# A chunked state-space layer: the inner matrices' transfers move from ScalarE to SyncE, and VectorE scans before it makes factors

## The reference, cut to what matters

```
u, z = split(h @ w_in, 2)                  # 512 x 2048 each
states = scan(lam_bar, b_bar @ u)          # 128 groups of 16 channels, 64 complex states each
y  = real(c @ states) + d * u
y  = gelu(y)
y  = y * sigmoid(y @ w_glu + b_glu)        # "glu"
out = (y * silu(z)) @ w_out
```

## Time and profile before

| | us |
|---|---|
| median of 3 runs | 1753.06 (1750.89 to 1755.3) |
| the profiled execution, its own time | 1754.76 |
| its span | 1752.8 |
| TensorE busy | 1678.9 (96%) |
| VectorE busy | 1008.3 (58%) |
| ScalarE busy | 676.2 (39%) |
| GpSimd busy | 590.2 (34%) |

### The profile page before, as it was taken

The page is one execution under the profiler, slowest core; times in us unless marked ns, Lnnn a source line. Parts: engine busy times, 40 slices in busy tenths (PEclk is TensorE's granted clock), DMA queues, the critical chain, the costliest instruction groups (busy, mean ns, idle before and its releaser), DMA issues.

```text
span 1752.8 us, 22905 instructions
## 1 busy us (share of the span) xinstructions
PE 1678.9 (96%) x9216; PEld 1341.5 (77%) x9216; DVE 1008.3 (58%) x1524; ACT 676.2 (39%) x965; POOL 590.2 (34%) x203
## 2 busy tenths in 40 slices
PE   7999999999999998999999999998999999999997
PEld 6777788888788886777788877686677788887876
DVE  4256545686988889985563654897963222222123
ACT  5473223334344355445333323425663322222122
POOL 1422013343633342000244432333774344443432
PEclk8999999999999999999999999998999999999999
DMA  5223002335655665555744322112002233332322
GB/s 165 83 96 96 1 11 89 95 96 143 154 119 136 139 141 106 105 115 163 244 135 128 88 70 73 48 43 85 2 1 73 79 90 96 96 96 74 100 83 81
DMA packets 267566, 168.14 MB, mean 96 GB/s; under 512 B 88875, under 2 KB 247814, under 8 KB 267334
## 3 DMA queue, kind: packets, MB, share of 16 engines
q1 hardware_dynamic: 240544, 142.80, 30.2%
q10 hardware_dynamic: 26614, 22.25, 4.8%
q0 software_dynamic: 304, 1.65, 0.3%
HBM read 145.15 MB, written 16.78 MB: 92 GB/s over the span
## 4 chain that ended last, share of the span: by engine, by line
PE 79%; DVE 11%; ACT 3%; issue 2%; DMA 2%; ACTq 1%; POOL 1%; SPq 0%; DVEq 0%; POOLq 0%
PE PS L700 22%; PE PS L701 22%; PE PS L702 22%; DVE ring_lo L1960 2%; PE PA L896 1%; PE PA L893 1%; ACTq L1621 1%; PE PA L874 1%; PE PS L1260 1%; PE PS L1272 1%; PE PA L1106 1%; PE PA L1244 1%; POOL ring_lo L2639 1%; DVE PB L2563 1%; ACT ring_hi L1382 1%
## 5 line engine op out<-in xcount | busy, mean ns | idle before, releaser
L2639 POOL TENSOR_TENSOR ring_lo<-ring,ring_hi 128x2048 fp32r<-128x2048 f32 (+2 forms) x93 | 405.6, 4361 | 965.9 <-ACT ring_hi L1382 965.5
L1382 ACT ACTIVATE ring_hi<-ring 128x2048 fp32r<-128x2048 f32 (+2 forms) x123 | 223.2, 1821 | 209.5 <-PE PS L702 171.8
L700 PE MATMUL PS<-U3h,ring_hi 128*128 128x512 f32 x352 | 140.0, 398 | 3.1 <-POOL ring_lo L2639 3.1
L701 PE MATMUL PS<-U3l,ring_hi 128*128 128x512 f32 x352 | 140.6, 399 | 0.0
L702 PE MATMUL PS<-U3h,ring_lo 128*128 128x512 f32 x352 | 139.5, 396 | 0.0
L2599 DVE TENSOR_TENSOR SF<-PS,rs 128x512 f32<-128x512 f32 x22 | 15.2, 691 | 166.7 <-PE PS L702 166.6
L700 PE MATMUL PS<-HT5h,ring_hi 128*128 128x512 f32 x256 | 106.3, 415 | 3.0 <-DVE ring_lo L1960 2.9
L1960 DVE TENSOR_TENSOR ring_lo<-ring,ring_hi 128x2048 fp32r<-128x2048 f32 x30 | 91.6, 3065 | 27.6 <-ACT ring_hi L1382 27.6
L702 PE MATMUL PS<-HT5h,ring_lo 128*128 128x512 f32 x256 | 101.4, 396 | 0.0
L701 PE MATMUL PS<-HT5l,ring_hi 128*128 128x512 f32 x256 | 101.2, 395 | 0.0
L1870 ACT ACTIVATE SF<-SF 128x512 f32<-128x512 f32 x22 | 13.9, 632 | 179.1 <-DVE SF L2599 179.1
(11 more groups left out here) (486 smaller groups left out, 4224.9 us busy)
## 6 DMA issues: line engine op xcount, KB each, us to landing
ring<-in_gla_w_in SPq DMA_DIRECT2D x20, 1024.0 KB, 5.2
ring<-in_s_w_in SPq DMA_DIRECT2D x16, 1024.0 KB, 5.8
ring<-in_s_w_glu SPq DMA_DIRECT2D x16, 1024.0 KB, 5.9
ring<-in_w_gate SPq DMA_DIRECT2D x22, 512.0 KB, 4.0
ring<-in_w_up SPq DMA_DIRECT2D x22, 512.0 KB, 5.3
ring<-in_w_down SPq DMA_DIRECT2D x16, 704.0 KB, 4.4
ring<-in_w_in SPq DMA_DIRECT2D x9, 1024.0 KB, 5.2
ring<-in_gla_w_out SPq DMA_DIRECT2D x8, 1024.0 KB, 5.8
```

Source lines behind the costliest of these rows:

```text
L700: pe.matmul(dst, w[0], x[0], start=start, stop=False)
L701: pe.matmul(dst, w[0], x[1], start=False, stop=False)
L1382: act.activation(ring_hi[:, n % NSLOT, 0:plan.size[n]], ring[:, n % NSLOT, 0:plan.size[n]], ACT.Copy)\
L2639: pool.tensor_tensor(ring_lo[:, n % NSLOT, at], ring[:, n % NSLOT, at], ring_hi[:, n % NSLOT, at].bitcast(F32), ALU.subtract).then_inc(wlo ...
```

## The change

ScalarE keeps the 8 issues for batch 0. For batches 1 to 15 they move into a new function `inner_rows(b)` of SyncE, first in `beside_batch(b)`, ahead of `u_loads(b + 1)` and `factor_loads(b + 3)`, with the waits that ScalarE had. VectorE scans first; `b_factors(b + 2)` now stands behind the low parts and the second tile, ahead of the state factors. In batch 15 TensorE has the second tile (`glu_a` 11) whole before `outputs(15)`, and half of `glu_a` 12 between `outputs(15)` and `by_feature(15)`. The instructions are the same in kind and number.

```diff
--- before.py
+++ after.py
@@ -1037,17 +1037,20 @@
                 if b == GA + 2:
                     by_feature(b - 1)
 
-                k = KD if b == GA + 1 else 6
+                k = KD if b in (GA + 1, NBATCH - 1) else 6
                 dense(*beside[1], 0, k)
                 outputs(b)
                 if b + 1 < NBATCH:
                     inside(b + 1)
+                else:
+                    dense(*S5_LAST[0], 0, 4)
                 dense(*beside[1], k, KD)
                 if b != GA + 1:
                     by_feature(b)
                 if len(beside) > 2:
                     dense(*beside[2], 0, KD)
-            for stage, m in S5_LAST:
+            dense(*S5_LAST[0], 4, KD)
+            for stage, m in S5_LAST[1:]:
                 dense(stage, m, 0, KD)
             for i, tile in enumerate(tiles["s5_glu"]):
                 w = parts_view(tile.loads[0], (KD, 2 * P))
@@ -1612,13 +1615,12 @@
                     ins = act.activation(GS[0:SGRP].rearrange("p (r q) m -> p q r m", q=4)[:, q],
                                          PA[32 * q:32 * q + SGRP, 1, 0:2 * P].rearrange("p (r m) -> p r m", r=2), ACT.Copy)
                 ins.then_inc(gs_ready, 1)
-                act.wait_ge(gs_ready, b + 1)
+
                 if b == 0:
+                    act.wait_ge(gs_ready, 1)
                     act.wait_ge(km_zero, 2)
-                if b >= 2:
-                    act.wait_ge(y_ps, b - 1)
-                for t in range(TB):
-                    act.dma_start(KM[b % 2][t * SGRP:(t + 1) * SGRP, :, t * SGRP:P], GS[0:SGRP, :, 0:P - t * SGRP]).then_inc(km_in[b % 2], 16)
+                    for t in range(TB):
+                        act.dma_start(KM[0][t * SGRP:(t + 1) * SGRP, :, t * SGRP:P], GS[0:SGRP, :, 0:P - t * SGRP]).then_inc(km_in[0], 16)
 
             def outputs_of(b):
 
@@ -2306,8 +2308,6 @@
             dve.wait_ge(xt_out, 16)
             link(dve.memset(M[:].rearrange("p g n -> p (g n)"), 0.0))
             for b in range(NBATCH):
-                if b + 2 < NBATCH:
-                    b_factors(b + 2)
                 scan(b)
                 own_tiles = [tile for tile in BESIDE[b] if tile[0] != "glu_a"]
                 for tile in own_tiles[:1]:
@@ -2324,6 +2324,8 @@
                     low_weights(n)
                 for tile in own_tiles[1:2]:
                     scaled(*tile)
+                if b + 2 < NBATCH:
+                    b_factors(b + 2)
                 if b + 2 in DVE_STATES:
                     state_factors(b + 2)
                 for tile in own_tiles[2:]:
@@ -2722,8 +2724,20 @@
                 for s in range(TB):
                     sp.dma_start(UB[s * SGRP:(s + 1) * SGRP, b % 2], src[s]).then_inc(ub_in[b % 2], 16)
 
+            def inner_rows(b):
+
+                sp.wait_ge(gs_ready, b + 1)
+                if b == 1:
+                    sp.wait_ge(km_zero, 2)
+                if b >= 2:
+                    sp.wait_ge(y_ps, b - 1)
+                for t in range(TB):
+                    sp.dma_start(KM[b % 2][t * SGRP:(t + 1) * SGRP, :, t * SGRP:P], GS[0:SGRP, :, 0:P - t * SGRP]).then_inc(km_in[b % 2], 16)
+
             def beside_batch(b):
 
+                if b >= 1:
+                    inner_rows(b)
                 if 1 <= b and b + 1 < NBATCH:
                     u_loads(b + 1)
                 if b + 3 < NBATCH:
```

## The result

| | before | after |
|---|---|---|
| median of the runs, us | 1753.83 (8 runs) | 1746.72 (8 runs, 1740.12 to 1749.51) |
| ratio to before | | 0.9955, 95% interval 0.9941 to 0.9969 |
| span of the profiled execution | 1752.8 | 1744.1 |

The change made the kernel faster by 0.45%, 7.9 us by the ratio. The forecast was 1744.1 us, 9.0 less than before.

A forecast was written before the change was run, and what follows sets the result against it. TensorE, busy 96% of the span, was taken as the bound, with VectorE setting the pace from scan 9. Gains of 7.4 us to `outputs(14)` and 1.6 in batch 15 gave 1753.06 - 9.0 = 1744.1 us; eight-in-ten range 1740 to 1751.5.

The forecast's parts named there:

- Batches 0 to 7: Factors no longer stand ahead of the scan, so TensorE's waits for `M` and low parts go: 4.5 us gained.
- The covers: Factors made late in loop b are ready 2.2 us (even b) and 3.3 us (odd b) before batch b + 1 wants them.
- The new wait: Batch 8 to 9: factors of batch 10 meet GpSimd's last state factors, so TensorE waits 3.9 us.
- The chain of VectorE: Scan 9 to 14: both rotation waits go, leaving 98.2 us of work, plus 3.8 for a fifth factor set: 102.0.
- The clock: After the 3.9 us of idling TensorE loses 1.3 us to the lower clock; 0.65 us reach the chain.
- That rival: Clock stays down longer: TensorE loses 4.3 us, the last `z` tile holds VectorE 3.7; gain 5.9, 1747.2 us; chance 0.12.
- Batch 15: Rotations and scan in time, six more matmuls before `outputs(15)`: the 1.46 us wait goes, 1.6 us gained.
- The sum on 9.0: 7.4 us gained up to `outputs(14)` plus 1.6 in batch 15 make 9.0 us.
- ScalarE's relief is hidden: Rival: copies and rotations late from other work, so waits of 5.5 and 1.6 stay; gain 1.9, 1751.2 us; chance 0.08.
- Inner matrices late: Rival: `KM` takes 10 us in SyncE's queue, four even batches wait 3.1 us each; 1756.5 us; chance 0.05.
- Factors late everywhere: Rival: two more GpSimd meetings delay factors before `b_to_rows(b + 1, 0)`, batches 1 to 8; 14.8 us lost, 1758.9; chance 0.11.

The follow-up runs named there:

- e6: The whole change, but VectorE instead of GpSimd makes the state factors of batch 10; median 1741.50 us, ratio to before 0.9929.
- e5: The whole change, but the factors of batch 10 stand ahead of scan 8; median 1742.12 us, ratio to before 0.9926.
- e1: Against before, only the 8 issues of `KM` move from ScalarE to SyncE; median 1748.01 us, ratio 0.9962.
- e2: Against before, only VectorE's order changes: scan first, factors of b + 2 behind the second tile; median 1748.84 us, ratio 0.9971.
- e4: The whole change without its TensorE part in the last batch; median 1746.66 us, ratio to before 0.9958.
- e7: The whole change, but SyncE issues `KM` behind `UB` and the factors' inputs; median 1760.48 us, ratio to before 1.0036.
- e8: The whole change, but VectorE makes the first two factor instructions twice in loops 0 to 7; median 1760.88 us, ratio to before 1.0032.
- e9: e5, but ScalarE makes the first product of `turns` for batches 11 to 15; `turns` moves behind the low parts; 1738.00 us, ratio to before 0.9907.
- e3: Against before, only TensorE's last batch changes; median 1752.17 us, ratio 0.9992.

## Why the prediction was right, point by point

All measured times count from `additions(0)`; predicted ones are those of the prediction.

| step | predicted | measured |
|---|---|---|
| batches 0 to 7, gain | 4.5 | 4.4 at `additions(8)` |
| wait before `b_to_rows(10, 0)` | 3.9 | 3.84 |
| scan 9, in the times of before | 671.4 | 671.65 |
| wait before `b_to_rows(11, 0)` | 4 to 5 | 4.32 |
| VectorE's wait for the `z` tile | 0.65 | 1.04 |
| scan 9 to scan 14 | 102 to 103 | 103.3 |
| gain at `outputs(14)` | 7.4 | 6.6 |
| gain in batch 15 | 1.6 | 1.8 |
| sum | 9.0 | 8.4 |

- **Batches 0 to 7** went as written: no wait for `M`, none for low parts, none for factors. The covers were 1.7 to 2.8 and 3.6 to 4.0 us where I had 2.2 and 3.3. But the argument that GpSimd's pieces "are mostly over" when the factors come did not hold: the factors met them in every one of these loops, for 1.6 to 3.3 us each time.
- **The new wait** was the step with the most in it, a meeting with GpSimd put into a new place, and it came out to 0.1 us. e6 shows the cause by taking GpSimd away, e5 shows that it lay on the path.
- **The chain of VectorE** held: the sum 98.2 + 3.8 was right. Its story was not, as e1 and e2 showed. I wrote that both waits for rotations go because ScalarE is relieved, and that a set of factors is then added. With the relief alone (e1) both waits go too, but TensorE passes on only about 1.1 us of the second; with the order alone (e2) the added set fills it.
- **The clock** was undersized: TensorE lost 1.6 us behind the first wait, where I took 1.3, and 0.4 us more reached the chain than the 0.65. That rival's price, 3.7, was not reached in any profile, but e4 came to 2.2.
- **Batch 15** had the right size, by luck, and the wrong cause. I gave it to the rotations and six more matmuls together; the relief gives 1.6, the matmuls 0.2.
- **The sum on 9.0** is 0.6 us above the stretch. The term that was mis-sized is the clock's: 1.04 us reached VectorE where 0.65 stood. The rest is 0.25 each for the start of scan 9 and for the loops behind it, against 0.2 more in batch 15.
- **ScalarE's relief is hidden:** refuted by e1. Its price was wrong as well: with the issues still on ScalarE (e2) the rest gained 4.5 us in the stretch, not 1.9. The Trainium skill, DMA: Bandwidth & Descriptors, section Issuing engines are not separate DMA queues, says that starting DMAs from several engines saves only the sequencer's time, "usually small relative to the DMA itself". The measurement differs: ScalarE was waited for, and moving 5.2 us of issues per batch to SyncE was worth 6.6 us by the median, 3.8 in the profile (e1).
- **Inner matrices late:** by e7, the issues of batch 2 could have started 5.4 us later without a wait, and the rival that decided "from 6.9 us on" would have decided earlier, since I had left the landing out of it. It was also priced too low: each such wait was followed by a slow clock and cost 1.6 to 2.8 us more than itself.
- **Factors late everywhere:** did not happen, but e8 shows that it was nearer than its point of 2.2 us. 2.5 us more per loop cost 14 us, the 14.8 that the rival had, by another way: lateness carried on, not single waits. That the sizes agree is luck.

## What to carry to other kernels

Ask of each wait which engine has the chain, and add up that engine's work loop by loop: a wait on another engine is then a symptom, and work moved off the pacing engine is worth its full length (0.72 us a loop in e9), up to the slack of the next. When two edits remove waits on the same chain, their gains need not be a sum: one may fill the idle time that the other removes, and a wait that is gone is worth only what the next engine can follow. And a cover is not a slack per batch if lateness is handed on: what is to be spared is the engine's idle time per loop, here 0.5 us, and not the distance to its next customer, here 1.7 to 4.0 us.

## What the runs showed of the hardware

- Three GpSimd instructions with inputs in SBUF (128x1024, 2.03 us where nothing stood in their way) cost VectorE 5.1 us in two-input instructions beside them: 7.97 against 4.49 us for the same two, 2.82 against 1.21 for the next.
- A TensorE wait of 3.8 us was followed by a stretch at 1.2 GHz in each of after, e2 and e4; the delay that VectorE then saw was 1.04, 1.20 and 2.18 us. Shorter waits went either way. Those of 2.00 us in batch 0 of e1 and 2.19 us in batch 11 of e3 were followed by a granted clock of 0.76; those of 1.73 and 2.27 us in batches 0 and 9 of before and of 1.42 us in e5 were followed by 1.00.
- Eight DMA issues of 8 to 64 KB held ScalarE's queue for 5.1 to 6.7 us and SyncE's for 5.1 to 7.0; eight small activations of 128x65 took 2.03 us.
